# Weight sums moved within the recurrence, four early products on their own weight places, residual rows in pieces: a decoder block in float32 on one core

## The reference, cut to what matters

```
h = RMSNorm(x)
[q,k,v,g | x_rnn,gate_rnn | m_ret,m_rnn] = h @ W_in                 # 1024 x 10240
y_ret = (silu(g) * HeadNorm(Retention(rot(q), rot(k), v))) @ W_ret_o # 2048 x 1024
y_rnn = (RG_LRU(CausalDWConv4(x_rnn)) * gelu(gate_rnn)) @ W_rnn_o
x = x + (sigmoid(m_ret) * y_ret + sigmoid(m_rnn) * y_rnn) @ W_out    # 1024 x 1024
h = RMSNorm(x); up = CausalDWConv3(h @ W_up)                         # 1024 x 5632
x = x + (silu(gate) * val) @ W_down                                  # 2816 x 1024
out = RMSNorm(x)
```

## Time and profile before

| | us |
|---|---|
| three runs | 2001.58, 2000.24, 1995.85; median 2000.24 |
| the profiled execution | 2002.64, of which span 2001.0 |
| PE busy | 1954.9 (98%), 8776 matmuls |
| PE busy in 100:200, 200:300, 300:400, 400:500, 500:600 | 100.00, 92.72, 97.03, 95.63, 98.43 |
| PE busy in 1300:1400 | 93.17 |
| PE busy in 0:100 and 1900:2001 | 90.64 and 94.24 |
| DVE / ACT / POOL busy | 1444.7 (72%) / 936.7 (47%) / 339.9 (17%) |
| mean granted PE clock | 0.994 of 2.4 GHz |

### The profile page before, as it was taken

The page is one execution under the profiler, slowest core; times in us unless marked ns, Lnnn a source line. Parts: engine busy times, 40 slices in busy tenths (PEclk is TensorE's granted clock), DMA queues, the critical chain, the costliest instruction groups (busy, mean ns, idle before and its releaser), DMA issues.

```text
span 2001.0 us, 23787 instructions
## 1 busy us (share of the span) xinstructions
PE 1954.9 (98%) x8776; PEld 1613.3 (81%) x8776; DVE 1444.7 (72%) x1657; ACT 936.7 (47%) x1186; POOL 339.9 (17%) x285
## 2 busy tenths in 40 slices
PE   8999899999999999999999999998999999999998
PEld 6888777877788888878888788786788888888887
DVE  7877777778754555547777657988988788776766
ACT  6433244333444555545555443356544544543335
POOL 2000001000185000037776002200000000000000
PEclk9999999999999999999999999999999999999999
DMA  6343545555589532275666654631222222156533
GB/s 257 121 164 136 199 160 184 177 193 174 198 300 352 216 136 106 90 235 169 211 182 210 242 193 162 244 126 69 100 84 84 82 75 95 68 186 233 202 99 132
DMA packets 223324, 332.37 MB, mean 166 GB/s; under 512 B 12433, under 2 KB 146961, under 8 KB 222993
## 3 DMA queue, kind: packets, MB, share of 16 engines
q1 hardware_dynamic: 199488, 241.23, 36.6%
q0 software_dynamic: 23760, 90.18, 11.4%
HBM read 226.51 MB, written 104.86 MB: 166 GB/s over the span
## 4 chain that ended last, share of the span: by engine, by line
PE 67%; DVE 16%; DMA 7%; ACT 4%; issue 3%; SPq 2%; POOL 1%; DVEq 0%; ACTq 0%; POOLq 0%
PE ps L358 22%; PE ps L360 22%; PE ps L359 22%; DVE wx L2218 2%; DMA raw<-w_in 2%; DMA tq<-w_out 1%; SPq L613 1%; DMA scr_o<-tq 1%; DMA scr_t<-tq 1%; DVE ost L2312 1%; DMA stg<-scr_y 1%; DVE tt L2180 1%; DVE ws L341 1%; DMA raw<-scr_q 1%; PE ps L1281 1%
## 5 line engine op out<-in xcount | busy, mean ns | idle before, releaser
L1575 ACT ACTIVATE wx<-raw 128x1024 fp32r<-128x1024 f32 (+1 forms) x152 | 137.2, 905 | 267.9 <-DVE raw L2194 144.0
L358 PE MATMUL ps<-xs,wx 128*128 128x512 f32 x612 | 239.8, 392 | 5.9 <-DVE xs L2644 3.4
L359 PE MATMUL ps<-xs,wx 128*128 128x512 f32 x612 | 238.9, 390 | 0.0
L360 PE MATMUL ps<-xs,wx 128*128 128x512 f32 x612 | 238.7, 390 | 0.0
L358 PE MATMUL ps<-sc,wx 128*128 128x512 f32 x448 | 176.9, 395 | 16.2 <-ACT ub L1610 16.2
L2218 DVE TENSOR_TENSOR wx<-raw,wx 128x1024 fp32r<-128x1024 f32 (+1 forms) x152 | 157.6, 1038 | 30.1 <-ACT wx L1575 29.7
L359 PE MATMUL ps<-sc,wx 128*128 128x512 f32 x448 | 176.0, 393 | 0.0
L360 PE MATMUL ps<-sc,wx 128*128 128x512 f32 x448 | 175.9, 393 | 0.0
L358 PEld LDWEIGHTS ps<-xs,wx 128*128 128x128 f32 x612 | 115.1, 188 | 33.0 <-issue 4.8
L1610 ACT ACTIVATE ub<-ps 128x512 f32<-128x512 f32 x112 | 66.0, 596 | 161.5 <-PE ps L360 158.9
L360 PEld LDWEIGHTS ps<-xs,wx 128*128 128x128 f32 x612 | 115.3, 188 | 24.1
(11 more groups left out here) (297 smaller groups left out, 4773.7 us busy)
## 6 DMA issues: line engine op xcount, KB each, us to landing
raw<-w_in SPq DMA_DIRECT2D x80, 512.0 KB, 5.3
scr<-ost POOLq DMA_DIRECT2D x32, 1024.0 KB, 5.1
raw<-w_up SPq DMA_DIRECT2D x44, 512.0 KB, 4.2
tq<-w_down SPq DMA_DIRECT2D x88, 128.0 KB, 2.3
scr_t<-tq POOLq DMA_DIRECT2D x22, 512.0 KB, 3.2
scr_h<-vt POOLq DMA_DIRECT2D x11, 1024.0 KB, 4.3
tr<-w_ret_o SPq DMA_DIRECT2D x64, 128.0 KB, 4.2
scr_q<-tr POOLq DMA_DIRECT2D x16, 512.0 KB, 5.3
```

What stands on the lines that cost most here:

```text
L358: pe.matmul(out, w(HI), x(HI), start=first, stop=False, skip_group_check=True)
L359: pe.matmul(out, w(HI), x(LO), start=False, stop=False, skip_group_check=True)
L360: return pe.matmul(out, w(LO), x(HI), start=False, stop=last, skip_group_check=True)
L1575: act.activation(dst, src, ACT.Copy).then_inc(sem["f_hi"], 1)
```

## The change

Three edits, cut to their core:

1. **W_out's sums.** The 8 pieces leave the input projection. They get a tile of their own, `wq`, on the place of `graw`, and are loaded, combined and stored by `load_wq`, `combine` and `store_wq`: two in each of the recurrence's steps 1, 2 and 3, one before tile 0 and one before tile 5 of the read-back. The next step's `graw` waits for their stores.
2. **The passage.** Product 0 and product 1 of blocks 0 and 1 read their weights from a place of their own, `bx`, split during the out projection; for this, block 1's raw weights are loaded earlier and the last ten chunks of W_out go through a new place `rwo`. The order is now products (0,0), (1,0), (0,1), then the transposes (features 4 to 7 first), then (1,1). DVE's and ACT's orders follow.
3. **Loads and order.** Rows 4 to 7 of x are loaded one by one at chunks 31 to 34. `reto_w(4)` and `reto_w(5)` stand ahead of y21a and y21b. Some DVE operations of the out projection change places.

```diff
-WO_AT = list(range(8, 24, 2))
+WO_TILES = 8
+WO_AT = [[], [0, 1], [2, 3], [4, 5, 6, 7]]
...
+    wq, _ = at("wq", [P, 4, BC], F32, C + 16 * K1)
+    rwo, _ = at("rwo", [P, 2, 2, HALF], F32, e)
+    bx, _ = at("bx", [P, 2, 2, 2, 4, P], F32R, A + 80 * K1)
...
-    ORDER01 = [(0, 0), (0, 1), (1, 0), (1, 1), (0, 2), ...
+    ORDER01 = [(0, 0), (1, 0), (0, 1), (1, 1), (0, 2), ...
...
+            def load_wq(j):
+                k, cols = j // 2, j % 2 * BC
+                sp_.wait_ge(sem["tq_out"], 16 * (W_TILES + j))
+                for slot, r, h in ((0, 1, 1), (1, 0, 1), (2, 0, 0), (3, 1, 0)):
+                    row, col = (r * O_KT + k) * P, h * HALF + cols
+                    sp_.dma_start(wq[:, slot, :], w_o[row:row + P, col:col + BC]).then_inc(sem["tq_in"], 16)
...
+                if WO_AT[n - 1] and n:
+                    sp_.wait_ge(sem["tq_out"], 16 * (W_TILES + WO_AT[n - 1][-1] + 1))
                 for q, w in enumerate((w_a, w_i)):
                     sp_.dma_start(graw[...
...
+                for j in WO_AT[n][:2]:
+                    sp_.wait_ge(sem["gw_sp"], n + 2)
+                    load_wq(j)
...
             for t in range(KT):
+                if t in (0, 5):
+                    load_wq(WO_AT[-1][2 + t // 5])
                 sp_.wait_ge(sem["ys_sp"], t + 1)
...
+            reto_w(4)
             reto_y(2, 0, 0, 0, 4, "y21a")
+            reto_w(5)
             reto_y(2, 0, 0, 4, 8, "y21b")
...
-                if i == R_CHUNKS + 1:
+                t = i - R_CHUNKS + 1
+                if 4 <= t < 8:
...
-                    sp_.dma_start(x1[:, 4:8, :], x_t[:, 4:8, :]).then_inc(sem["x_re"], 16)
-            sp_.wait_ge(*late_count("rw_lo", R_CHUNKS + O_CHUNKS))
-            load_up(1, 1)
+                    sp_.dma_start(x1[:, t, :], x_t[:, t, :]).then_inc(sem["x_re"], 16)
+                if t in (8, 10):
+                    load_up(1, 1, [t // 2 - 4])
...
# PE
-            part(0, 0, 0)
+            part(0, 0, 0, w=bx[:, 0, 0])
+            pe.wait_ge(sem["x1_done"], 13)
+            part(1, 0, 1, w=bx[:, 1, 0])
...
-            part(0, 1, 0)
+            part(0, 1, 0, w=bx[:, 0, 1])
...
-            for k, bank in ((0, 4), (1, 5), (2, 2), (3, 3), (4, 6), (5, 7)):
+            for k, bank in ((4, 2), (5, 3), (6, 6), (7, 7), (0, 5)):
+                turn2(k, 1, bank)
+            for k, bank in ((1, 2), (2, 3), (3, 6)):
+                pe.wait_ge(sem["a22_in"], k)
                 turn2(k, 1, bank)
             pe.wait_ge(*late_count("s3_f", 1))
...
+            part(1, 1, 1, w=bx[:, 1, 1])
...
# ACT
+            act.wait_ge(sem["f_pr"], produced(1, 1) + W_P)
             s_hi(S1, s1f, lambda c: act.wait_ge(sem["s1_f"], c + 1))
...
# DVE, recurrence
+                for j in WO_AT[n][:2]:
+                    combine(wq, W_TILES + j)
                 dve.wait_ge(sem["tanh_done"], 4 * n + 4)
...
+                    if t in (1, 7):
+                        combine(wq, W_TILES + WO_AT[-1][2 + t // 7])
...
# DVE, out projection and passage
-            for t in range(4):
+            reto_last(0)
+            reto_last(1)
+            out_lo(i + 1)
+            for t in range(2, 4):
                 reto_last(t)
-            out_lo(i + 1)
...
+            out_lo(i + 8)
             out_s4(1)
-            out_lo(i + 8)
...
-            combine_t13(0, 0)
-            combine_t2(0, 0)
-            prep_lo(0, 0, "b1")
+            first_b1_lo(1)
             combine_t4(0, 0)
...
+            combine_t13(1, 1)
+            norm2(5)
+            combine_t2(1, 1)
+            combine_t4(1, 1)
             s_lo(A12, a12f, 0, 3)
...
+            s_lo(S2, a22f, 0, 7)
+            combine_s1(0)
+            s_lo(S2, a22f, 1, 8)
+            prep_lo(0, 0, "t13")
             s_lo(S1, s1f, 0, 9)
+            combine_s1(1)
```

More of the change, by code:

```diff
@@ L635, in _ @@
                                   ).then_inc(sem["a21_st"], 16)
-                for n in range(W_ALL):
-                    if W_SEQ[n][0] == b - 1:
-                        load_tq(n)
+                if b - 1 in W_AT:
+                    load_tq(W_AT.index(b - 1))
                 if b == LAST_XR + 3:
@@ L828, in mix_next @@
                 mix_load(sp_, g + 4)
-            for i in range(4, R_CHUNKS):
+            for i in range(6, R_CHUNKS):
                 reto_w(i)
@@ L989, in _ @@
             for b in range(IN_BLOCKS):
-                for n in range(W_ALL):
-                    if W_SEQ[n][0] == b:
-                        store_tq(n)
+                if b in W_AT:
+                    store_tq(W_AT.index(b))
                 if b >= R_BLOCK:
@@ L1000, in _ @@
                 for half in range(2):
+                    if half < len(WO_AT[n]):
+                        store_wq(WO_AT[n][half])
                     store(i, half, tokens[:, 4 * half:4 * half + 4, n * VD:(n + 1) * VD])
@@ L1774, in normalise, with first_b1_hi @@
                                bias=hn[:, slot, 12:13]).then_inc(sem["on_done"], 1)
+            def first_b1_hi(b):
+                act.wait_ge(fraw[b], 32)
+                act.activation(bx[:, b, :, HI, :, :], raw_half(b, M0), ACT.Copy).then_inc(sem["f_hi"], 1)
             def reto_w_hi(i):
@@ L1903, in _ @@
                 act.activation(a12f[:, k, :], ps[:, k, :], ACT.Copy, scale=gcol[4 + k]).then_inc(late_sem("a12_in"), 1)
+            norm2(5)
             act.wait_ge(sem["x1_st"], 32)
             s_hi(A12, a12f, lambda c: act.wait_ge(*late_count("a12_in", 2 * c + 2)))
-            for t in range(5, 8):
+            for t in range(6, 8):
                 norm2(t)
@@ L1910, in _ @@
             prep_hi(0, 0, "t2")
+            act.wait_ge(sem["f_t4"], 2 + W_T)
+            act.wait_ge(sem["x1_st3"], 16)
+            act.wait_ge(sem["xn_done"], 12)
+            act.activation(t4x[:, HI, :, :], raw_view(1)[:, 4:8, M0], ACT.Copy).then_inc(sem["f_hi"], 1)
             def copy_u(b, u, which):
@@ L2355, in _ @@
                 if b in W_AT:
-                    combine_tq(W_SEQ.index((b, 1, W_AT.index(b))))
+                    combine(tq, W_AT.index(b))
             a_p = prm[:, PRM["a_param"]:PRM["a_param"] + 8]
@@ L2625, in out_add @@
                 dve.wait_ge(sem["o_ps"], 4 * p + 2 * q + 2)
-                dve.wait_ge(sem["x_re"], 16 * half + 16)
+                dve.wait_ge(sem["x_re"], 80 if half else 16)
                 t, bank, cols = 4 * half + 2 * q, O_BANK[p] + 2 * q, slice(n * HALF, (n + 1) * HALF)
@@ L2651, in _ @@
             mixed(11)
-            for t in range(4):
+            reto_last(0)
+            reto_last(1)
+            out_lo(i + 1)
+            for t in range(2, 4):
                 reto_last(t)
-            out_lo(i + 1)
-            for n in range(12, 16):
-                mixed(n)
+            mixed(12)
+            mixed(13)
             out_lo(i + 2)
+            mixed(14)
+            mixed(15)
             out_s3(0)
@@ L2686, in _ @@
             out_lo(i + 11)
+            first_b1_lo(0)
             norm2(0)
@@ L2711, in _, with combine_s2, combine_s1 @@
             prep_lo(0, 0, "t2")
[L2712 to L2713 removed]
+            prep_lo(1, 1, "t4")
             dve.wait_ge(*late_count("neg_in", 1))
             def combine_s3(k):
[L2718 to L2719 removed]
+                dve.wait_ge(sem["tr_ps"], 20 + k + 1)
+                dve.scalar_tensor_tensor(out=s3f[:, k, :], in0=ps[:, (5, 2, 3, 6)[k], :], scalar=neg_g[:, k:k + 1],
                                          in1=a11f[:, k, :], op0=ALU.mult, op1=ALU.add).then_inc(late_sem("s3_f"), 1)
[L2722 to L2724 removed]
+            def combine_s2(c):
+                k = slice(2 * c, 2 * c + 2)
+                dve.wait_ge(*late_count("s3_f", 2 * c + 2))
+                dve.wait_ge(sem["xs_lo"], 5 + c)
+                dve.tensor_tensor(a22f[:, k, :], a22f[:, k, :], s3f[:, k, :], ALU.subtract).then_inc(sem["s2_f"], 1)
+            for k in range(4):
                 combine_s3(k)
[L2726 to L2727 removed]
             s_lo(A22, a22f, 0, 5)
             s_lo(A22, a22f, 1, 6)
[L2730 to L2736 removed]
+            combine_s2(0)
+            combine_s2(1)
+            def combine_s1(c):
                 k = slice(2 * c, 2 * c + 2)
```

123 lines of the change are left out of this document (53 added, 70 removed).

## The result

| | us, median | all runs |
|---|---|---|
| kernel before | 2000.9 | 1995.9 to 2002.7 (4) |
| changed kernel | **1976.3** | 1975.5 to 1977.1 (4) |
| predicted | 1971.0 | 1963 to 1982 |

The ratio of the times is 0.9881 (95%: 0.9862 to 0.9900). The profiled executions took 2002.64 and 1976.1. So the change takes off 26.5 us where the sum said 30.6.

A forecast was written before the change was run, and what follows sets the result against it. PE is busy 98%, so time comes only from its stalls and half-clock stretches; 22.6 + 0 - 2.0 + 3.7 + 1.6 + 4.7 = 30.6 off 2002.64 gives 1972.0, forecast as a median of 1971, range 1963 to 1982.

The forecast's parts named there:

- Input projection, 22.6: Eight stalls on `ub` go, 17.5 us, and two low-clock stretches behind them, 5.1: a gain of 22.6 us.
- reserve of 0.3 to 0.8 us: Input projection: VectorE gets 2.4 us earlier against stalls of 1.6, leaving 0.8 on the mean, some 0.3 at the largest.
- first rival: Input projection: VectorE is the next bound, seven stalls keep 1 us each and one low-clock stretch stays: 1980; chance 0.12.
- Recurrence, 0: Steps 1 to 3: two rounds of pieces hide in VectorE's 27.49 us idle before tanh, 7 to 11 us to spare: 0.
- Read-back, -2.0: The second piece's issues and 512 KB go ahead of tile 5: a loss of 2.0 us, bounds 0.8 and 4.
- SP is free at about 855.6, so tile 5 is issued at 857.4 rather than 856.6: Read-back: the second piece's four issues in front of tile 5 delay its issue by 0.8 us, the low bound.
- The read-back costs more: Rival: both pieces' transfers lengthen tiles 3, 5, 7, and a second low-clock stretch comes: 5 more, 1976 to 1978; chance 0.07.
- the prediction's own sign: Wrong if PE still waits for `ub` in the input projection, or a stall over 3 us stands between 620 and 1400.
- W_ret_o, 3.7: Chunk 4's load ahead of y21a lands in time: 2.0 us of stall and 1.7 at low clock gained, bounds 0 and 3.7.
- W_out, 1.6: Two waits for VectorE, 0.7 and 0.6, go with 0.16 each: gain 1.6 us, bounds -1 and 2.2.
- Passage, 4.7: Before the up projection: stalls fall from 7.1 to 4.1 us, and 1.7 at low clock goes; bounds 1 and 8.
- the low-clock stretch, 1.7: Passage: 1.7 us lost at the lower clock counted as gained within 4.7; low bound has it half the times.

The follow-up runs named there:

- e1: Changed kernel with all edits of part 1 undone, the W_out sums back in the input projection on the shared tile: 1995.3 us.
- e11: Changed kernel with six small additions of 128x240 at the W_out sums' old place, ahead of the second tile sum, in the same eight blocks: 1976.5 us.
- e10: Changed kernel with two more VectorE operations of 1.2 us in each of eight input projection blocks, behind the second tile sum: 2000.2 us.
- e4: Changed kernel with the last W_out piece's load issued between tiles 5 and 6 of the read-back, not ahead of tile 5: 1972.9 us.
- e6: Changed kernel with the loads of W_ret_o's chunks 4 and 5 back behind the 1 MB loads y21a and y21b: 1977.3 us.
- e3: Changed kernel with two W_out pieces in each of the recurrence's four steps and none beside the read-back: 1971.4 us.
- e12: Changed kernel with the edits of e3 and e9 together: 1968.8 us.
- e9: Changed kernel with S1's second-half sum and t13's split moved earlier in the passage, and A12's split ahead of block 1's sums t2 and t4: 1973.1 us.
- e7: Changed kernel with VectorE's order in W_out's chunks 28 to 36 as before the change: 1976.5 us.
- e5: Changed kernel with the passage to the up projection as before (weights' place, transposes' order, ACT's and VectorE's order): 1978.8 us.

## Why the prediction was right, and where not

**Input projection, 22.6: right, and for its reason.** Measured 22.6; e1 brings the stalls back. That it is met to 0.1 is luck: of the 5.1 for the low clock only 4.2 were PE's, since the first stretch began 1.8 us before the first stall ended, and short gaps behind the stalls made up the other 0.9. e11 shows that the W_out sums themselves were not the loss, which leaves the waits for loads behind VectorE's tile sums. The reserve of 0.3 to 0.8 us was right as well (e10: 0.5). That makes the first rival a near miss: less than half of one more 1024-column operation in each pair of blocks fills the reserve.

**Recurrence, 0: right, to 0.3.** In step 1 the second round's sum ends at 675.8 and VectorE stands until 689.5:

```profile
674.23 0.69 DVE L2353 TENSOR_TENSOR wq<-wq 128x512 f32<-128x512 f32 x1 [8.60 <-DMA wq<-w_out]
...
689.55 2.29 DVE L2434 SCALAR_TENSOR_TENSOR th<-ea,th 128x2048 f32<-128x2048 f32 x1 [13.71 <-ACT ri L1755]
```

13.7 us were left where 7 to 11 were forecast. The recurrence's first wait scatters from kernel to kernel, from none (e4, e6) to 1.2 us, and 2.4 in e1, which has no piece there; no run shows why.

**Read-back, -2.0: the number was met by luck, and the mechanism was wrong.** The step that failed is "SP is free at about 855.6, so tile 5 is issued at 857.4 rather than 856.6". It took the store of the first piece to be out of the way after 0.8 + 3.2 us, a landing seen in the input projection. Here the stores landed in 7.1 (median over the recurrence and the read-back), and the one that matters in 8.0. Chain of the changed kernel:

```profile
828.92 8.01 DMA scr_o<-wq
837.32 1.21 SPq L628
...
840.11 4.23 DMA stg<-scr_y
...
846.79 3.23 DMA stg<-scr_y
...
853.42 3.33 DMA qkv<-scr_v
```

Since the second piece uses the same `wq`, SyncE stood until 836.9 for the landing, and the four issues took 3.05 us more, so tile 5 went out at 840.1. Its landing then took 4.23 us, less than the 5.52 of the earlier trace rows: the bytes ahead of it did not lengthen it. The delay came from the wait for a landing in the issuing queue. Counted back from PE's need of the first chunk, tile 5 went out some 6 us later than before, and the chunk's load 3.3 us later (issued at 852.48 against 871.56, where PE was ready for it at 855.6 and 878.0). The forecast had tile 5 issued 0.8 us later. Most of this was taken up by room that the chain had: the stalls grew by only 0.7 us, from 0.3 for `qkvs` and 2.2 for `ktm` to one of 3.2 for `qkvs`. The other 1.3 us are the low clock, 3.0 instead of 1.7, for which the forecast had no term; the rival "The read-back costs more" foresaw a second such stretch. By the prediction's own sign, a stall over 3 us between 620 and 1400, this place fails (3.0 as the view prints it, 3.2 from start to start). By the medians the two pieces beside the read-back cost 4.9 us (e3 against the changed kernel) and 4.3 (e12 against e9). That is more than the table's 2.0, since this stage lost anything from 0.1 (e3) over 3.3 (e12) to 4.4 us (e1, the kernel before) without pieces in it; so the 2.0 of one pair of traces is no firm price.
The Trainium skill ("DMA: Bandwidth & Descriptors", section Queues, rings and completion order) has the descriptors of one queue taken in order by each DMA engine; no lengthening by it, estimated at 1.2 us, can be seen in tile 5. The loads of chunk 4 behind two of 1 MB, 12.22 us in the earlier trace rows and 12.08 in e6, agree with it.
Why stores land later beside the read-back stays open. What the trace shows is that the packets of this store began about 4.5 us after its issue, while those of w_rnn_o's weights, 1 KB each, were on their way; the same tile's stores in the recurrence are slow too.

**W_ret_o, 3.7: right, in this execution.** Measured 3.8, no stall. Of the 3.7, 1.9 come with the stall each time (e6), and 1.7 only where the clock goes down behind it.

**W_out, 1.6: wrong, 0.0.** The step "`out_lo` of chunks 29 and 36 moves ahead of 1.1 to 2.3 us of other VectorE work" is so, but what it moved ahead of was not what held it up. VectorE in the changed kernel:

```profile
1247.37 2.30 DVE L2634 TENSOR_TENSOR ysr<-mq,ysr 128x1024 fp32r<-128x1024 f32 x1
...
1250.79 3.17 DVE L2596 TENSOR_TENSOR mq<-msg,mrb 128x512 f32<-128x512 f32 x2
1253.89 1.21 DVE L2517 TENSOR_TENSOR wsr<-raw,wsr 128x1024 fp32r<-128x1024 f32 x1
1255.03 1.21 DVE L2634 TENSOR_TENSOR ysr<-mq,ysr 128x1024 fp32r<-128x1024 f32 x1
```

Beside POOL's products these operations take about twice their time (2.30 against 1.21 for the first), now one chunk later: stalls of 0.79 and 0.51 us at chunks 29 and 30 became three of 0.62, 0.35 and 0.22 at chunks 30 to 32. At chunk 36 PE waits for `out_add`, which frees the banks, and this was not moved ahead. The Trainium skill's rule on VectorE beside GpSimd ("SBUF — State Buffer", section Who interferes with whom) agrees with the doubling; the 0.8 worked out from it was nearer than the 1.6 that I took.

**Passage, 4.7: right in kind, 2.7.** Each stall was forecast at its place: 1.0 for A12 (measured 1.25), 0.8 and 2.0 for S1 (0.87 and 1.93), none for the transposes. Without the clock the gain is 2.7 where 3.0 were forecast. The term that failed is "the low-clock stretch, 1.7", counted as gained: it came back in this kernel, in e7, e10 and e11 (in e1 with 6.8 us), and stayed away behind the same stalls in e3, e4 and e6. And where it stayed away only 0.5 us came of it, since PE then waits for `wx` (e6): a gain of 3.2 in all, not 4.7.

**The sum.** The miss of the profiled executions, 4.1 us, is 1.6 in W_out, 2.0 in the passage and 0.3 in the recurrence, with 0.2 of small differences elsewhere. The median I put 1.0 under the profiled sum (before, it lay 1.7 to 2.4 under it); this kernel's lay 0.2 above it. That makes the median's miss of 5.3.

## What to carry to other kernels

Idle time on an engine is a reserve only for work that stands ahead of the event which ends it; behind that event the same microseconds cost in full (2.6 us free at one place, 2.5 us at the other 24 us in eight blocks). A transfer that waits for a store's landing puts that landing into the issuing queue, so take the landing from the stage in which it will happen, and give a second piece a place of its own or an issue behind what is urgent. Put a stretch at low clock into a forecast by its chance, and ask what PE meets next when the stretch is gone: here 1.7 us of work saved were 0.5 us of time. And when stalls and low clock are added up from a trace, take care that what overlaps is not counted twice; the starts of the same instructions in two traces give the gain without that risk.

## What the runs showed that was not expected

The same stalls of 0.87 and 1.93 us before product (0,4) were followed by 3.4 us at 1.2 GHz in some kernels and by none in others, though the products around them were the same. In the read-back each single stall of 2.2 to 4.4 us (both kernels, e5 to e11) came with 3.4 or 6.8 us at the lower level, and the split ones of 1.5 + 2.6 (e1), 1.6 + 2.1 (e4) and 1.6 + 1.3 (e12) with none. By these traces, one of each kernel, two short stalls can be cheaper than one as long as both; no run was made to test it. Kernels with eight stalls in the input projection also seem to scatter more from one execution to the next (the kernel before 10 us in 19, e1 12 and e10 5 in 10) than those without (under 4 in 4 each). In e1 the granted clock goes with the time: 0.994 in the slowest execution and 0.997 in the fastest.
